# The last units of two projections, taken one block of tokens at a time, with the norm behind them

## The chip, the cores and the metric

The kernel runs on one core of a Trainium2 chip. Its time is the device time of one execution in microseconds (us); lower is better. TensorE (PE) multiplies, VectorE (DVE) and ScalarE (ACT) work on vectors, GpSimd (POOL) does a few of them and issues some transfers, SyncE (SP) issues the large ones.

## The reference, cut to what matters

An encoder of two layers over 256 tokens of width 1024, in float32. Each layer has a mixer (three branches, gated and merged) and a feed-forward part: dense in layer 0, eight experts with top-2 routing in layer 1. What matters here is where the residual x is completed and normalised:

```python
for l in range(DEPTH):
    h = rmsnorm(x, g_mix[l])
    ...
    x = x + merged @ w_o[l]
    h = rmsnorm(x, g_ffn[l])
    if l % 2 == 0:
        x = x + swiglu(h, ffn_w1[i], ffn_w3[i], ffn_w2[i])
    else:
        x = x + moe_ffn(h, moe_router[i], moe_w1[i], moe_w3[i], moe_w2[i])
return rmsnorm(x, g_final)
```

`rmsnorm` divides each token by the root of its mean square over 1024 features and multiplies by a gain.

## The kernel before

**Data.** X holds the residual, tokens on the 128 partitions, in two blocks of tokens (b = 0, 1) with 1024 columns each, which are handled in two halves of 512. Each matrix product is made of three (`mm3`): operands are split into a rounded part (`hi`) and a remainder (`lo`), and hi*hi, hi*lo and lo*hi are added up. Weights come in units of 1 MB (512 rows by 512 columns as a rule; the last of the dense stage have 256 rows). SyncE loads unit u into one of 4 raw buffers when unit u-4 is done (`unit_done`), ScalarE rounds it (L782, `whi`, 3 buffers, so it waits for unit u-3), VectorE makes the remainder (L1132, `wlo`), TensorE multiplies. Each engine follows its own list in order; the semaphores between them are written by hand, and so is the place of every step in each list.

**Units.** Layer 0's mixer has units 0 to 33, the last four of which are w_o: halves 0 and 1 of the first 512 rows (30, 31), then of the other 512 (32, 33). Units 34 to 69 are the dense stage: six steps of 512 hidden columns (256 in the last), w1 and w3, then w2, one step behind; units 68 and 69 are the two halves of the last w2. Unit 70 is the first of layer 1's mixer, whose last four are w_o again. After them the expert stage has a ring of its own.

**The last two units.** `token_unit` (L1679) multiplies one unit for block 0 and then for block 1: the order at the end of w_o is unit 32 for block 0, unit 32 for block 1, unit 33 for block 0, unit 33 for block 1. With `tell` it counts `first_block` after block 0. VectorE adds each of the four sums (b, half) to X (L1438 for w_o, L1465 for the dense stage) and counts `x_ready`, half 0 for both blocks first.

**Norm.** ScalarE squares the four parts of X with a sum (L798); VectorE adds the two halves of the sums (L1148), ScalarE takes the root (L802), VectorE the reciprocal (L1150), each in one instruction for both blocks. VectorE scales block 0 into xn in two parts (L1156), ScalarE block 1 (L809). TensorE turns xn with transposes (L1726), 8 tiles for each block, the two blocks of a tile one after the other, into PSUM (`small`, where the dense stage's sums lie too), counting `norm_turned` after each two tiles. ScalarE rounds the turned tiles with the gain (L816), VectorE makes the remainders (L1170), and the next stage's products can start. `busy(n)` (L1741) issues n products of identity and table whose result nobody reads, which fill time in which TensorE has nothing to do:

```python
if n == 2:
    pe.wait_ge(fh_ready, FSTEPS)
    busy(3, big[1][:, 1, :])
    pe.wait_ge(x_ready, 8)
```

norm(1) follows layer 0's w_o, norm(2) the dense stage. Between the last units and the adds VectorE makes, by its list, the remainder of the unit after them (34, or 70). When layer 0's w_o is added, GpSimd writes 16 blocks of zeros of 512 KB to memory (it waits for `x_ready` 4); after the dense stage it issues layer 1's small loads (`x_ready` 8).

**Before the experts.** After layer 1's w_o, X itself is turned (16 transposes, L1726; fillers `busy(1)` before them), ScalarE and VectorE copy the turned tiles with the gain in turn (L1072 and L1480), and TensorE multiplies them by the router (L1991). Routing and the gathering of tokens follow, and then the first expert unit. The squares for norm(3) are taken by ScalarE around those copies (L1066).

Of the kernel before, what the change touches and what calls it, by code (L numbers as in the profile page):

```python
# [188 lines left out]
def encoder(nc, ins, out):  # L189
    ctx = ExitStack()  # L190
    with ctx:
# [217 lines left out]
        xn_ready = [sem(f"xn_ready{b}") for b in range(NB)]  # L409
        xg_ready = sem("xg_ready")  # L410
# [239 lines left out]
        def _(pool):  # L650
# [46 lines left out]
            for b in range(NB):  # L697
                pool.wait_ge(xn_ready[b], 7)
                pool.tensor_tensor(xn[:, b, :], xn[:, b, :], gffn[:, :], ALU.mult).then_inc(xg_ready, 1)
# [49 lines left out]

        def norm_place(n, k):  # L750
# [20 lines left out]
        def _(act):  # L771
# [14 lines left out]
            def norm_stats(n, ready=None, count=0):  # L786
# [275 lines left out]
            def squares(half):  # L1062
                for b in range(NB):
                    act.wait_ge(x_ready, 8 + 2 * half + b + 1)
# [10 lines left out]
            act.wait_ge(var_ready, 4)  # L1075
# [18 lines left out]
            def last_scale(b):  # L1094
                act.wait_ge(var_ready, 4 + b + 1)
# [19 lines left out]
        def _(dve):  # L1115
# [20 lines left out]
            def norm(n, gain=None):  # L1136
# [10 lines left out]
                dve.wait_ge(ss_ready, n + 1)  # L1147
                dve.tensor_tensor(nvar[:, n, :], nss[:, n, 0, :], nss[:, n, 1, :], ALU.add).then_inc(var_ready, 1)  # L1148
                dve.wait_ge(sd_ready, n + 1)
                dve.reciprocal(nrs[:, n, :], nsd[:, n, :]).then_inc(rs_ready, 1)  # L1150
                dve.wait_ge(rs_ready, n + 1)
# [67 lines left out]

            def mixer(l):  # L1220
                u0 = l * LAYER0_UNITS
                norm(2 * l, R_MIX + KD * l)
# [208 lines left out]
                for g in (G_O, G_O + 1):  # L1431
                    for b in range(NB):
                        if b == 0:
                            dve.wait_ge(first_block, 4 * l + g - G_O + 1)
                        else:
                            dve.wait_ge(unit_done, group_end(l, g))
                        part = X[:, b, 512 * (g - G_O):512 * (g - G_O) + 512]
                        dve.tensor_tensor(part, part, big[g % 2][:, b, :], ALU.add).then_inc(x_ready, 1)  # L1438

            def dense():  # L1440
                norm(1, R_FFN)
# [16 lines left out]
                for half in range(2):  # L1458
                    for b in range(NB):
                        if b == 0:  # L1460
                            dve.wait_ge(first_block, 2 + half + 1)
                        else:
                            dve.wait_ge(unit_done, LAYER0_UNITS - 1 + half)
# [679 lines left out]
```

## Time and profile before

| | us |
|---|---|
| median of 3 runs | 1650.73 |
| lowest, highest | 1650.01, 1652.11 |
| profiled execution | 1649.36 |
| its span, first to last instruction | 1647.7 |
| TensorE busy | 1623.6 (99%) |
| VectorE busy | 1253.3 (76%) |
| ScalarE busy | 1045.6 (63%) |
| mean granted TensorE clock | 0.996 |

The span is the time from the first to the last instruction of one profiled execution; busy times are shares of it. The granted clock is the share of full speed that the chip gave TensorE. A timeline lists instructions in order of start, several of one line merged (x4), and in brackets the idle time of the engine before them with the instruction that ended it.

### The profile page before, as it was taken

The page shows a single profiled execution, that of the slowest core. Times are in us where ns is not written, and L with a number is a line of the kernel's source. Part 1 is how long each engine was busy: PE and PEld are TensorE (multiplying, and loading weights), DVE is VectorE, ACT ScalarE, POOL GpSimd, SP SyncE. Part 2 cuts the span into 40 slices and gives each one's busy share as a digit, 9 for nine tenths or more (in the row PEclk, how much of TensorE's full clock was granted, in tenths as well). Part 3 has the DMA queues.
Part 4 walks back from the last instruction along what each step waited for, and adds up shares of the span by engine and source line. Part 5 has one row for each costly group of instructions (what it writes and reads, how often), then busy time and mean ns, then how long its engine had stood idle before and what let it go on. Part 6 is the DMA issues. An engine that isn't in the chain of part 4 may idle for free.

```text
span 1647.7 us, 22770 instructions
## 1 busy us (share of the span) xinstructions
PE 1623.6 (99%) x8939; PEld 1400.6 (85%) x8939; DVE 1253.3 (76%) x929; ACT 1045.6 (63%) x927; POOL 118.6 (7%) x92
## 2 busy tenths in 40 slices
PE   8999999999999999999999999999999999999998
PEld 6899989999898999777888888888888888888886
DVE  5755575454557567699888898888988988988996
ACT  4464645433534564676777776877776876877775
POOL 1000002000000000022100100100100000001450
PEclk8999999999999999999999999999999999999999
DMA  7644459554754446999999999999999999999980
GB/s 265 200 148 136 153 182 355 187 194 143 243 179 150 142 145 212 412 359 408 387 399 361 390 387 368 393 382 368 398 377 364 401 379 363 404 376 366 415 354 26
DMA packets 162622, 488.98 MB, mean 297 GB/s; under 512 B 8192, under 2 KB 12512, under 8 KB 162560
## 3 DMA queue, kind: packets, MB, share of 16 engines
q1 hardware_dynamic: 154416, 459.05, 75.2%
q0 software_dynamic: 7552, 27.89, 4.7%
q10 hardware_dynamic: 592, 1.16, 0.2%
q8 instruction: 45, 0.74, 0.2%
q14 instruction: 17, 0.14, 0.0%
HBM read 471.82 MB, written 16.25 MB: 296 GB/s over the span
## 4 chain that ended last, share of the span: by engine, by line
PE 91%; DVE 4%; ACT 2%; DMA 2%; issue 1%; POOL 0%; ACTq 0%; DVEq 0%; POOLq 0%
PE big L1675 21%; PE big L1677 21%; PE big L1676 21%; PE small L1675 7%; PE small L1677 7%; PE small L1676 7%; PE small L1726 2%; DVE elo L1217 2%; DMA raw<-ffn_w 1%; ACT ehi L985 1%; ACT whi L782 1%; PE big L1726 1%; DMA lqk<-diff_lk 0%; PE small L1975 0%; DVE wlo L1132 0%
## 5 line engine op out<-in xcount | busy, mean ns | idle before, releaser
L1217 DVE TENSOR_TENSOR elo<-eraw,ehi 128x2048 fp32r<-128x2048 f32 x336 | 774.5, 2325 | 97.4 <-ACT ehi L985 94.5
L985 ACT ACTIVATE ehi<-eraw 128x2048 fp32r<-128x2048 f32 x336 | 641.7, 1918 | 239.9 <-PE big L1677 136.4
L1132 DVE TENSOR_TENSOR wlo<-raw,whi 128x2048 fp32r<-128x2048 f32 (+2 forms) x104 | 230.0, 2218 | 191.7 <-ACT whi L782 191.6
L1675 PE MATMUL big<-ehi,hehi 128*128 128x512 f32 x896 | 351.5, 392 | 4.0 <-DVE elo L1217 3.4
L782 ACT ACTIVATE whi<-raw 128x2048 fp32r<-128x2048 f32 (+2 forms) x104 | 192.4, 1859 | 250.1 <-PE big L1677 177.3
L1677 PE MATMUL big<-ehi,helo 128*128 128x512 f32 x896 | 348.9, 389 | 0.0
L1676 PE MATMUL big<-elo,hehi 128*128 128x512 f32 x896 | 348.7, 389 | 0.0
L1675 PE MATMUL big<-hhi,whi 128*128 128x256 f32 x864 | 246.8, 286 | 2.2 <-DVE wlo L1132 0.8
L1677 PE MATMUL big<-hhi,wlo 128*128 128x256 f32 x864 | 244.5, 283 | 0.0
L1676 PE MATMUL big<-hlo,whi 128*128 128x256 f32 x864 | 244.4, 283 | 0.0
L1675 PEld LDWEIGHTS big<-ehi,hehi 128*128 128x128 f32 x896 | 168.2, 188 | 40.2 <-DVE elo L1217 4.5
L1677 PEld LDWEIGHTS big<-ehi,helo 128*128 128x128 f32 x896 | 168.2, 188 | 35.4
L1676 PEld LDWEIGHTS big<-elo,hehi 128*128 128x128 f32 x896 | 168.3, 188 | 34.0
L1675 PEld LDWEIGHTS big<-hhi,whi 128*128 128x128 f32 x864 | 165.7, 192 | 4.7 <-issue 2.0
L1676 PEld LDWEIGHTS big<-hlo,whi 128*128 128x128 f32 x864 | 165.8, 192 | 0.6 <-issue 0.5
L1677 PEld LDWEIGHTS big<-hhi,wlo 128*128 128x128 f32 x864 | 165.7, 192 | 0.0
L1675 PE MATMUL small<-ehi,eahi 128*128 128x512 f32 x384 | 150.2, 391 | 0.0
L1677 PE MATMUL small<-ehi,ealo 128*128 128x512 f32 x384 | 149.7, 390 | 0.0
L1676 PE MATMUL small<-elo,eahi 128*128 128x512 f32 x384 | 149.4, 389 | 0.0
L1677 PEld LDWEIGHTS small<-ehi,ealo 128*128 128x128 f32 x384 | 72.1, 188 | 15.2
L1676 PEld LDWEIGHTS small<-elo,eahi 128*128 128x128 f32 x384 | 72.1, 188 | 14.8
L1675 PEld LDWEIGHTS small<-ehi,eahi 128*128 128x128 f32 x384 | 72.1, 188 | 14.8
(353 smaller groups left out, 1766.0 us busy)
## 6 DMA issues: line engine op xcount, KB each, us to landing
eraw<-moe_w SPq DMA_DIRECT2D x336, 1024.0 KB, 6.3
raw<-ffn_w SPq DMA_DIRECT2D x30, 1024.0 KB, 5.0
raw<-w_gate SPq DMA_DIRECT2D x24, 1024.0 KB, 5.0
raw<-w_in SPq DMA_DIRECT2D x20, 1024.0 KB, 5.1
raw<-w_branch SPq DMA_DIRECT2D x12, 1024.0 KB, 5.0
raw<-w_o SPq DMA_DIRECT2D x8, 1024.0 KB, 5.1
xs_all<-zeros POOLq DMA_DIRECT2D x12, 512.0 KB, 8.8
xn<-xs_all POOLq DMA_DIRECT2D x8, 512.0 KB, 6.8
```

The source lines that it names most:

```text
L782: act.activation(whi[u % HI][:, 0:kt, 0:cols], raw[u % RAW][:, 0:kt, 0:cols], ACT.Copy).then_inc(hi_ready, 1)
L985: act.activation(ehi[HI_OF[n]][:, :], eraw[n % RING][:, :], ACT.Copy).then_inc(ehi_ready, 1)
L1132: dve.tensor_tensor(wlo[u % RAW][:, 0:kt, 0:cols], raw[u % RAW][:, 0:kt, 0:cols], whi[u % HI][:, 0:kt, 0:cols].bitcast(F32), ALU.subtract) ...
L1217: dve.tensor_tensor(elo[n % RING][:, :], eraw[n % RING][:, :], ehi[HI_OF[n]][:, :].bitcast(F32), ALU.subtract).then_inc(elo_ready, 1)
L1675: pe.matmul(o, sh, mh, start=start, stop=False, **kw)
L1676: pe.matmul(o, sh, ml, start=False, stop=False, **kw)
L1677: return pe.matmul(o, sl, mh, start=False, stop=stop, **kw)
L1726: return pe.transpose(o, src, ident[0:n, 0:n])
```

## The change

The last two units of w_o (both layers) and of the dense stage are multiplied by a new function, `token_pair`: block 0 for both halves, then block 1 for both halves. `first_block` is counted after each half of block 0 and `unit_done` after each of block 1, so that the first unit of a pair is counted as done after its second block. VectorE adds block 0's two halves to X first, then block 1's. In norm(1) and norm(2) the sum, the root, the reciprocal and the scaling are done for block 0 and then for block 1, on VectorE with the adds in between, and the adds are moved into `norm`. ScalarE scales one half of block 1, VectorE the other. TensorE turns all tiles of block 0, waits for all of X, issues two fillers in place of three, and turns block 1. Before the experts it turns block 0's tiles of X, the first five without waiting for block 1, and then block 1's; the filler there goes. Counts of semaphores follow.

```diff
@@ -788,25 +795,25 @@
                 act.activation(warm[:, n:n + 1], eps[:, :], ACT.Sqrt)
-                for half in range(2):
-                    for b in range(NB if n else 1):
+                for b in range(NB if n else 1):
+                    for half in range(2):
...
-                            act.wait_ge(ready, count + 2 * half + b + 1)
+                            act.wait_ge(ready, count + 2 * b + half + 1)
                         part = slice(512 * half, 512 * half + 512)
                         i = act.activation(xn[:, b, part], X[:, b, part], ACT.Square,
                                            accum_out=nss[:, n, half, b:b + 1])
-                i.then_inc(ss_ready, 1)
-                act.wait_ge(var_ready, n + 1)
-                act.activation(nsd[:, n, :], nvar[:, n, :], ACT.Sqrt, scale=1.0 / D, bias=eps[:, :]).then_inc(sd_ready, 1)
+                    i.then_inc(ss_ready, 1)
+                    act.wait_ge(var_ready, stat(n, b))
+                    of = slice(b, b + 1) if n else slice(0, NB)
+                    act.activation(nsd[:, n, of], nvar[:, n, of], ACT.Sqrt, scale=1.0 / D, bias=eps[:, :]).then_inc(sd_ready, 1)
...
             def norm(n, gain, ready=None, count=0):
-                    act.wait_ge(rs_ready, n + 1)
-                    for part in (slice(0, 512), slice(512, 1024)):
-                        act.activation(xn[:, 1, part], X[:, 1, part], ACT.Copy, scale=nrs[:, n, 1:2]).then_inc(xn_ready[1], 1)
+                    act.wait_ge(rs_ready, stat(n, 1))
+                    act.activation(xn[:, 1, 0:512], X[:, 1, 0:512], ACT.Copy, scale=nrs[:, n, 1:2]).then_inc(xn_ready[1], 1)
...
@@ -1059,9 +1066,9 @@
+            def squares(b):
+                for half in range(2):
+                    act.wait_ge(x_ready, 8 + 2 * b + half + 1)
                     part = slice(512 * half, 512 * half + 512)
                     i = act.activation(xn[:, b, part], X[:, b, part], ACT.Square, accum_out=nss[:, 3, half, b:b + 1])
                 return i
...
@@ -1144,17 +1151,33 @@
-                for part in (slice(0, 512), slice(512, 1024)):
-                    for b in range(1 if n else NB):
-                        dve.tensor_scalar(xn[:, b, part], X[:, b, part], nrs[:, n, b:b + 1], None,
-                                          ALU.mult).then_inc(xn_ready[b], 1)
...
+                else:
+                    for b in range(NB):
+                        for half in range(2):
+                            added(b, half)
+                        dve.wait_ge(ss_ready, stat(n, b))
+                        dve.tensor_tensor(nvar[:, n, b:b + 1], nss[:, n, 0, b:b + 1], nss[:, n, 1, b:b + 1],
+                                          ALU.add).then_inc(var_ready, 1)
+                        dve.wait_ge(sd_ready, stat(n, b))
+                        dve.reciprocal(nrs[:, n, b:b + 1], nsd[:, n, b:b + 1]).then_inc(rs_ready, 1)
+                        dve.wait_ge(rs_ready, stat(n, b))
+                        for part in (slice(0, 512), slice(512, 1024))[b:]:
+                            dve.tensor_scalar(xn[:, b, part], X[:, b, part], nrs[:, n, b:b + 1], None,
+                                              ALU.mult).then_inc((xn_ready[0], xn_late)[b], 1)
...
@@ -1217,9 +1240,31 @@
...
+            def mixed(l):
+                def add(b, half):
+                    if b == 0:
+                        dve.wait_ge(first_block, 4 * l + half + 1)
+                    else:
+                        dve.wait_ge(unit_done, group_end(l, G_O + half))
+                    part = X[:, b, 512 * half:512 * half + 512]
+                    dve.tensor_tensor(part, part, big[half][:, b, :], ALU.add).then_inc(x_ready, 1)
+                return add
+            def fed(b, half):
+                if b == 0:
+                    dve.wait_ge(first_block, 2 + half + 1)
+                else:
+                    dve.wait_ge(unit_done, LAYER0_UNITS - 1 + half)
+                part = X[:, b, 512 * half:512 * half + 512]
+                dve.tensor_tensor(part, part, small[:, 2 * b + half, :], ALU.add).then_inc(x_ready, 1)
...
@@ -1428,17 +1473,12 @@
-                for g in (G_O, G_O + 1):
                     for b in range(NB):
-                        if b == 0:
-                            dve.wait_ge(first_block, 4 * l + g - G_O + 1)
-                        else:
-                            dve.wait_ge(unit_done, group_end(l, g))
-                        part = X[:, b, 512 * (g - G_O):512 * (g - G_O) + 512]
-                        dve.tensor_tensor(part, part, big[g % 2][:, b, :], ALU.add).then_inc(x_ready, 1)
+                        for half in range(2):
+                            mixed(l)(b, half)
...
             def dense():
-                norm(1, R_FFN)
+                norm(1, R_FFN, mixed(0))
...
@@ -1676,7 +1708,21 @@
+            def token_pair(us, outs, ahi, alo, k0, first):
+                for b in range(NB):
+                    for half, u in enumerate(us):
+                        _, kt, cols = units[u]
+                        if b == 0:
+                            pe.wait_ge(lo_ready, u + 1)
+                        for k in range(kt):
+                            i = mm3(outs[half][b][:, 0:cols], ahi[:, k0 + k, b * P:b * P + P], alo[:, k0 + k, b * P:b * P + P],
+                                    whi[u % HI][:, k, 0:cols], wlo[u % RAW][:, k, 0:cols],
+                                    first and k == 0, k == kt - 1)
+                        i.then_inc((first_block, unit_done)[b], 1)
+            def token_unit(u, outs, ahi, alo, k0, first, last):
                 _, kt, cols = units[u]
...
@@ -1744,23 +1788,44 @@
             def norm(n):
+                if n == 2:
+                    pe.wait_ge(x_ready, 6)
+                elif n:
+                    wait_out(0, *(f"{n}{j}" for n in ("PV", "DT") for j in range(2)))
...
+                for k in range(KD):
+                    if k % 4 == 0:
+                        pe.wait_ge(xn_ready[0], 2 * n + 1 + k // 4)
+                    if n == 2 and k == 4:
+                        pe.wait_ge(x_ready, 8)
+                    turn(norm_place(n, k)[:, 0:P], xn[:, 0, k * P:k * P + P])
                 if n == 2:
                     pe.wait_ge(fh_ready, FSTEPS)
-                    busy(3, big[1][:, 1, :])
-                    pe.wait_ge(x_ready, 8)
-                elif n:
-                    wait_out(0, *(f"{n}{j}" for n in ("PV", "DT") for j in range(2)))
-                    busy(3)
+                else:
+                    pe.wait_ge(x_ready, 4)
+                busy(2, big[1][:, 1, :])
                 for k in range(KD):
-                    q, j = k // 2, k % 2
-                    if n == 0 and q == 3:
-                        pe.wait_ge(pcol_ready, 1)
-                    for b in range(NB):
-                        if k % 4 == 0:
-                            pe.wait_ge(xn_ready[b], 2 * n + 1 + k // 4)
-                        i = turn(norm_place(n, k)[:, P * b:P * b + P], xn[:, b, k * P:k * P + P])
-                    if j:
+                    if k == 0:
+                        pe.wait_ge(xn_ready[1], n + 1)
+                    if k == 4:
+                        pe.wait_ge(xn_late, n + 1)
+                    i = turn(norm_place(n, k)[:, P:2 * P], xn[:, 1, k * P:k * P + P])
+                    if k % 2:
                         i.then_inc(norm_turned, 1)
...
@@ -1935,13 +2000,14 @@
                 branch(l, 4)
                 pe.wait_ge(br_read[1], 3 * l + 2)
                 branch(l, 5)
-                for j in range(2):
-                    for g in (G_O, G_O + 1):
-                        if not j:
-                            pe.wait_ge(br_read[g % 2], 3 * l + 3)
-                        pe.wait_ge(mlo_ready, 2 * l + j + 1)
-                        token_unit(l * LAYER0_UNITS + group_units(g)[j], [big[g % 2][:, b, :] for b in range(NB)],
-                                   hhi, hlo, 4 * j, j == 0, j == 1, tell=bool(j))
+                for g in (G_O, G_O + 1):
+                    pe.wait_ge(br_read[g % 2], 3 * l + 3)
+                    pe.wait_ge(mlo_ready, 2 * l + 1)
+                    token_unit(l * LAYER0_UNITS + group_units(g)[0], [big[g % 2][:, b, :] for b in range(NB)],
+                               hhi, hlo, 0, True, False)
+                pe.wait_ge(mlo_ready, 2 * l + 2)
+                token_pair([l * LAYER0_UNITS + group_units(g)[1] for g in (G_O, G_O + 1)],
+                           [[big[half][:, b, :] for b in range(NB)] for half in range(2)], hhi, hlo, 4, False)
...
@@ -1957,10 +2023,15 @@
                     if f:
                         pe.wait_ge(flo_ready, f)
+                        if f == FSTEPS:
+                            token_pair([LAYER0_UNITS - 2, LAYER0_UNITS - 1],
+                                       [[small[:, 2 * b2 + half, :] for b2 in range(NB)] for half in range(2)],
+                                       fhi[(f - 1) % 2], flo[(f - 1) % 2], 0, False)
+                            continue
...
@@ -1979,12 +2050,13 @@
             dense()
             mixer(1)
             wait_out(1, *(f"{n}{j}" for n in ("PV", "DT") for j in range(2)))
-            busy(1)
-            pe.wait_ge(x_ready, 12)
+            pe.wait_ge(x_ready, 10)
             for k in range(KD):
-                for b in range(NB):
-                    i = turn(turned_place(k)[:, P * b:P * b + P], X[:, b, k * P:k * P + P])
-                i.then_inc(norm_turned, 1)
+                if k == 5:
+                    pe.wait_ge(x_ready, 12)
+                turn(turned_place(k)[:, 0:P], X[:, 0, k * P:k * P + P])
+            for k in range(KD):
+                turn(turned_place(k)[:, P:2 * P], X[:, 1, k * P:k * P + P]).then_inc(norm_turned, 1)
```

## Rows read from the trace of the kernel before

**Rows 1.** The page, busy time: us, share of the span, instructions.

```profile
PE 1623.6 (99%) x8939; PEld 1400.6 (85%) x8939; DVE 1253.3 (76%) x929; ACT 1045.6 (63%) x927; POOL 118.6 (7%) x92
```

**Rows 2.** TensorE's waits, 445 to 1640: us in total, times, longest.

```profile
PE big L1675 <- DVE elo L1217: 3.4, 4, 1.3
```

**Rows 3.** Timeline of TensorE, first seam: start, us, engine, line; in brackets idle before.

```profile
244.80 0.39 PE L1677 MATMUL big<-whi,hlo 128*128 128x512 f32 x1
...
245.03 2.73 PE L1744 MATMUL small<-tab 128*128 128x512 f32 x6
...
248.06 2.00 PE L1726 MATMUL small<-tab,xn 128*128 128x128 f32 x16 [0.30 <-DVE xn L1156]
...
250.29 0.36 PE L1675 MATMUL big<-hhi,whi 128*128 128x256 f32 x1 [0.23 <-DVE hlo L1170]
```

**Rows 4.** Timelines of VectorE, then ScalarE, first seam.

```profile
230.71 4.49 DVE L1132 TENSOR_TENSOR wlo<-raw,whi 128x2048 fp32r<-128x2048 f32 x2 [0.58 <-ACT whi L782]
...
239.79 0.69 DVE L1438 TENSOR_TENSOR X<-X,big 128x512 f32<-128x512 f32 x1 [0.54 <-PE big L1677]
...
245.23 0.69 DVE L1438 TENSOR_TENSOR X<-X,big 128x512 f32<-128x512 f32 x1 [2.03 <-PE big L1677]
...
247.43 0.96 DVE L1156 TENSOR_SCALAR xn<-X,nrs 128x512 f32<-128x512 f32 x2
...
247.43 1.33 ACT L809 ACTIVATE xn<-X,nrs 128x512 f32<-128x512 f32 x2 [0.23 <-DVE nrs L1150]
...
248.79 3.04 ACT L816 ACTIVATE hhi<-small,pcol 128x256 fp32r<-128x256 f32 x8
```

**Rows 5.** Windows: length, busy of each engine, TensorE clock, DMA share, GB/s.

```profile
245.00:246.00 1.00, 1.00 (x4) 0.49 (x3) 0.69 (x1) 0.05 (x1) 0.02 (x1) 1.00 0.00 0
...
278.00:280.00 2.00, 2.00 (x19) 2.00 (x18) 1.21 (x1) 1.40 (x2) 0.00 (x0) 1.00 1.05 407
```

**Rows 6.** Timeline of TensorE, dense stage, two waits.

```profile
274.36 0.35 PE L1675 MATMUL big<-hhi,whi 128*128 128x256 f32 x1 [0.77 <-ACT fsil L964]
...
281.14 0.39 PE L1675 MATMUL big<-hhi,whi 128*128 128x256 f32 x1 [0.80 <-DVE wlo L1132]
```

**Rows 7.** Timeline of TensorE, second seam.

```profile
440.11 2.73 PE L1744 MATMUL big<-tab 128*128 128x512 f32 x6
...
443.75 2.00 PE L1726 MATMUL small<-tab,xn 128*128 128x128 f32 x16 [0.91 <-DVE xn L1156]
...
445.98 0.36 PE L1675 MATMUL big<-hhi,whi 128*128 128x256 f32 x1 [0.23 <-DVE hlo L1170]
```

**Rows 8.** Timeline of VectorE, second seam.

```profile
436.87 2.29 DVE L1132 TENSOR_TENSOR wlo<-raw,whi 128x2048 fp32r<-128x2048 f32 x1 [5.07 <-ACT whi L782]
...
439.08 2.47 DVE L1465 TENSOR_TENSOR X<-X,small 128x512 f32<-128x512 f32 x4
...
442.39 0.16 DVE L1148 TENSOR_TENSOR nvar<-nss 128x2 f32<-128x2 f32 x1 [0.84 <-ACT xn L798]
...
443.12 0.88 DVE L1156 TENSOR_SCALAR xn<-X,nrs 128x512 f32<-128x512 f32 x2
```

**Rows 9.** Timelines of TensorE, then ScalarE, third seam.

```profile
667.86 1.02 PE L1744 MATMUL small<-tab 128*128 128x512 f32 x2
...
668.80 1.09 PE L1726 MATMUL small<-tab,X 128*128 128x128 f32 x8
...
670.70 3.62 PE L1991 MATMUL small<-hT,rt 128*8 128x256 f32 x16
...
669.27 0.91 ACT L1072 ACTIVATE hT<-small,pcol 128x256 f32<-128x256 f32 x2 [4.24 <-PE small L1726]
```

**Rows 10.** Start of the kernel: TensorE's timeline, then windows.

```profile
11.77 0.27 PE L1726 MATMUL big<-tab,prow 96*128 96x96 f32 x1 [4.37 <-DMA prow<-gm_b_s]
...
12.00:13.00 1.00, 0.66 (x2) 0.36 (x2) 0.60 (x4) 0.57 (x2) 0.00 (x0) 0.78 1.06 412
...
22.00:24.00 2.00, 1.82 (x12) 1.47 (x11) 2.00 (x6) 1.99 (x6) 0.00 (x0) 0.80 1.00 408
```

More of the change, by code:

```diff
@@ L1134, in split_to, with norm @@
                     split[0] += 1
-            def norm(n, gain=None):
+            def norm(n, gain=None, added=None):
                 if n == 0:
@@ L1146, in norm @@
                     dve.tensor_copy(rb4[:, :, :], bc(rb[:, :], 2, [BUCKETS, HEADS, P])).then_inc(rb4_ready, 1)
[L1147 to L1151, printed above, removed]
+                if n == 3 or n == 0:
+                    dve.wait_ge(ss_ready, stat(n, 0))
+                    dve.tensor_tensor(nvar[:, n, :], nss[:, n, 0, :], nss[:, n, 1, :], ALU.add).then_inc(var_ready, 1)
+                    dve.wait_ge(sd_ready, stat(n, 0))
+                    dve.reciprocal(nrs[:, n, :], nsd[:, n, :]).then_inc(rs_ready, 1)
+                    dve.wait_ge(rs_ready, stat(n, 0))
@@ L1457, in dense @@
                 split_to(LAYER0_UNITS)
-                for half in range(2):
-                    for b in range(NB):
[L1460 to L1463, printed above, removed]
-                        part = X[:, b, 512 * half:512 * half + 512]
-                        dve.tensor_tensor(part, part, small[:, 2 * b + half, :], ALU.add).then_inc(x_ready, 1)
             dve.memset(eps[:, :], EPS).then_inc(eps_ready, 1)
@@ L1677, in mm3 @@
                 return pe.matmul(o, sl, mh, start=False, stop=stop, **kw)
-            def token_unit(u, outs, ahi, alo, k0, first, last, tell=False):
+            def token_pair(us, outs, ahi, alo, k0, first):
+                for b in range(NB):
+                    for half, u in enumerate(us):
[8 more added lines that the diff above has]
+            def token_unit(u, outs, ahi, alo, k0, first, last):
                 _, kt, cols = units[u]
@@ L1747, in norm @@
                 if n == 2:
-                    pe.wait_ge(fh_ready, FSTEPS)
-                    busy(3, big[1][:, 1, :])
-                    pe.wait_ge(x_ready, 8)
+                    pe.wait_ge(x_ready, 6)
                 elif n:
                     wait_out(0, *(f"{n}{j}" for n in ("PV", "DT") for j in range(2)))
-                    busy(3)
-                for k in range(KD):
-                    q, j = k // 2, k % 2
-                    if n == 0 and q == 3:
-                        pe.wait_ge(pcol_ready, 1)
-                    for b in range(NB):
-                        if k % 4 == 0:
-                            pe.wait_ge(xn_ready[b], 2 * n + 1 + k // 4)
-                        i = turn(norm_place(n, k)[:, P * b:P * b + P], xn[:, b, k * P:k * P + P])
-                    if j:
+                if n == 0:
+                    for k in range(KD):
+                        if k == 6:
+                            pe.wait_ge(pcol_ready, 1)
+                        for b in range(NB):
+                            if k == 0 or (k == 4 and b == 0):
+                                pe.wait_ge(xn_ready[b], 1 + k // 4)
+                            elif k == 4:
+                                pe.wait_ge(xn_late, 1)
+                            i = turn(norm_place(n, k)[:, P * b:P * b + P], xn[:, b, k * P:k * P + P])
+                        if k % 2:
+                            i.then_inc(norm_turned, 1)
+                    return
+                for k in range(KD):
+                    if k % 4 == 0:
[4 more added lines that the diff above has]
+                if n == 2:
+                    pe.wait_ge(fh_ready, FSTEPS)
+                else:
[7 more added lines that the diff above has]
+                    i = turn(norm_place(n, k)[:, P:2 * P], xn[:, 1, k * P:k * P + P])
+                    if k % 2:
                         i.then_inc(norm_turned, 1)
```

29 lines of the change are left out of this document (16 added, 13 removed).

## The prediction

> **What bounds the kernel now.** I read the page's busy shares first, then its chain, then TensorE's waits, and last the timelines of the three places that the change touches. TensorE is busy for 99% of the span [rows 1], and the chain runs along it nearly throughout. After the second place TensorE hardly waits for anyone until the end: the largest wait from there on is 3.4 us in four pieces, on expert weight remainders [rows 2]. So a microsecond lost before TensorE's next long run of products is lost at the end, unless a later transfer is what TensorE would have waited for. The three places are the seams at which the residual X is completed. Seam 1 (norm(1), after layer 0's w_o): the last product is issued until 245.03, fillers and turns follow, and the first dense product starts at 250.29 [rows 3], 5.26 us later. Seam 2 (norm(2), after the dense stage): 440.11 to 445.98, 5.87 us [rows 7]. Seam 3 (X turned for the router): 667.86 to the first router product at 670.70, 2.84 us [rows 9].
>
> **Seam 1, on TensorE's side.** The products are the same ones in another order. Block 0's sums are then complete two half units earlier, while block 1's last sum still completes at the same moment, so its add still starts at 245.23 and block 1's scale is ready at 247.43, 2.20 us after it [rows 4]. Block 0's whole chain lies under products: its second add started at 239.79 before and still can, its scale is there 2.20 us later at 241.99, and two scaled parts take 0.96 us [rows 4], done before 243, with 2 us to spare. The weight remainder of the last unit is needed 2.7 us earlier (half a unit of 24 products, which are issued 0.23 us apart [rows 3]), and both remainders are done at 235.20 [rows 4] against a need at 245.03 - 8.16 = 236.87: a margin of 1.7 us. What is left after 247.43: ScalarE makes one scaled copy in place of two (1.33 us for two, so 0.67), ready at 248.10. TensorE turns block 0 and runs two fillers in the meantime. The step from a ready part to a turn took 0.15 us (247.43 + 0.48 to 248.06), and at seam 3 two turns released ScalarE 0.47 us after they started (668.80 to 669.27) [rows 3, 4, 9], which gives 248.72 for ScalarE's first rounding, against 248.79 now. Most of what the seam loses in turns was already hidden behind ScalarE's second copy, so the gain is 0.1 us.
>
> **Seam 1, what comes after.** Even that is not kept. When X is complete GpSimd writes 16 blocks of zeros of 512 KB, and the 16 DMA engines are then full: share 1.05 still at 278 to 280 us [rows 5]. TensorE waits in that stretch at 274.36 (0.77 us, for ScalarE, which had stood before it for a weight block to land) and at 281.14 (0.80 us) [rows 6]. TensorE's position at 281 is thus set by bytes queued from 247 on. Unit 36's load is released by unit 32, which counts as done 2.7 us later than before, but the DMA engines are idle at 245 to 246 [rows 5], and that transfer fits there. I take 0 for seam 1, between -0.2 and +0.2.
>
> **Seam 2.** Here the cover is missing. VectorE makes the remainder of unit 70 first (436.87 to 439.08, it waits for ScalarE, which waits for a unit that ends as before), and only then adds to X. Before, the four adds ran in one go (2.47 us, 0.62 each), ScalarE's squares beside them, and one chain of sum, root and reciprocal led to the scale at 443.12 [rows 8]. In the changed order VectorE takes block 0 alone: adds at 439.08 and 439.70, then it stands still in `norm` for ScalarE's square, for the root and for its own reciprocal, with block 1's adds queued behind those waits. Scale of block 0 at 439.70 + 2.20 = 441.90, two scaled parts 0.88, so block 1's adds at 442.78 and 443.40, and its scale at 443.40 + 2.20 = 445.60: 2.48 us later than 443.12. Then ScalarE's copy, 0.67, 446.27. TensorE turns block 0's first four tiles at about 442.5, waits for all of X (443.40 + 0.68 = 444.08) before the other four because they land where block 1's products lie, and runs two fillers of 0.91 us (a third of 2.73 [rows 7]), until about 446.5. Block 1's turns start at 446.5, ScalarE's rounding at 446.97 against 444.45 now (443.12 + 1.33, the two copies of [rows 4]), and the first product moves from 445.98 to about 448.5: +2.5 us. Low end +1.8 (the rounding starts as soon as the one copy is done, 446.27 against 444.45), high end +3.0 (all eight turns of block 1, 1.0 us, stand before it in place of two). Nothing behind it takes it back [rows 2].
>
> The Trainium skill (TensorE: Matmul & The Clock Gate, Architectural detail) says that ScalarE and VectorE are strictly first in, first out. The trace agrees: VectorE stood for 0.84 us before its sum at 442.39 [rows 8]. Were the engine able to pass a waiting instruction, seam 2 would cost nothing and the sum would be -0.5 us.
>
> **Seam 3.** Turns of block 0 now start with the last product, at 667.86; five are done when block 1's last add ends (667.86 + 5 x 0.12 = 668.5 against 668.80, when turns could start before). Three of block 0 and eight of block 1 remain: 11 in place of 16, and 16 took 1.90 us [rows 9], so 0.12 each and 1.31 in all. Router products then start at 668.80 + 1.31 = 670.11 in place of 670.70: -0.6 us at most. The copies of the turned tiles start some 0.3 us later than 669.27, and the first router product needs one, 0.47 us long, so it starts at 670.0 to 670.2. I take -0.5, between -0.6 and 0 (0 if the copies, in pairs of 0.46 us, set the pace). VectorE's routing and the first expert unit follow that chain. The filler of 0.94 us that goes stood beside the wait for X and costs nothing.
>
> **The rest.** Two more sums, roots and reciprocals on one column each, all of them inside the chains above. Layer 1's small loads, which GpSimd issues when X is complete, start 2.5 us later; the middle of the layer wants them.
>
> **Sum.** 0 + 2.5 - 0.5 = +2.0 us, own bounds +1.0 (-0.2 + 1.8 - 0.6) to +3.2 (0.2 + 3.0). The profiled execution took 1649.36 us (span 1647.7), so it would be 1651.4; it is 1.4 us under the median of the runs, 1650.73, so the median comes to 1652.7, with 1651.7 to 1653.9 as its own range.
>
> **Rivals.**
> A, the slower side: the clock falls at seam 2. Before, three fillers followed the last product at once. Now TensorE is empty from 440.11 to 442.5 (2.4 us), turns for 0.5, is empty for 1.1, works 3.3 and is empty for 1 more. In this trace TensorE's granted clock fell from the upper level (2.4 GHz) to the lower (1.2 GHz) between 12 and 13 us, after it had done nothing from 7.4 to 11.77, and came back only between 22 and 24 [rows 10]. Against it: expert stage gaps of 1.3 us cost no clock, and 2.4 is much shorter than 4.4. Price: 0 to half of that stretch of some 10 us, 4.9; I take 2.5, so +4.5 and 1655.2 us. It decides from 2.6 us at the lower level on (1.3 us lost, which with +2.0 passes 3.3). Chance 0.2. The Trainium skill (same page, What's actually happening) has the array throttled by default and activity releasing it; by that alone the thin seam would fall to the lower level, and the sum would be the same +4.5.
> B, faster than before: block 0's chain is covered at seam 2 as well, the case that makes all three seams shorter. It would need block 1's last add at 440.31, 0.2 after the last product; counting back through one add (0.62), two parts (0.88) and 2.20, block 0's second add at 436.6 and VectorE free at 436.0. Unit 70's remainder would have to be done 3.1 us earlier, and [rows 8] show it starting at 436.87. Price: the seam falls from 5.87 to seam 1's 5.26 less 0.1, so -0.7; with -0.5 and up to -0.1 that is -1.3, and 1649.4 us. Chance 0.06.
> C, seam 3 gives nothing (copies set its pace) and seam 2 its high end: +3.0, 1653.7 us. Chance 0.1, next to the forecast and inside its range.
>
> **How the numbers follow.** A measurement of this kernel tells about 0.2% from no change, 3.3 us here, so slower begins at 1654.0 and faster ends at 1647.4. The forecast holds 0.60 and C 0.10, together 0.62 within and 0.08 above. A's 0.20 is 0.18 above and 0.02 within. B's 0.06 lies within. 0.04 is left, set on faster, for a cover at seam 2 together with a gain further on that no row shows. Same 0.70, slower 0.26, faster 0.04. Range: 1649.3 takes B in, 1656.5 most of A.
>
> **What would show it.** Right: in the trace after, first product of layer 1 some 8.3 us after the last dense product (5.87 before), VectorE's adds at seam 2 in two pairs with about 2.5 us between them, block 1's scale 2.5 us later; first dense product 5.1 to 5.3 us after w_o's last, and TensorE's waits near 274 and 281 still there; first router product 2.2 to 2.4 us after the last of w_o. Wrong: four adds in one run at seam 2, or unit 70's remainder out of the way before them, or a granted clock under 1 near 440 to 455.

## The result and the profile after

The changed kernel takes 1653.83 us (median of 12 runs, 1651.62 to 1655.66), the kernel before 1650.33 us (12 runs beside them). The ratio is 1.0021, 95% interval 1.0013 to 1.0028: +3.5 us, between +2.1 and +4.6. The interval does not hold 1, so the changed kernel is slower; by 0.21%, which is at the 0.2% where the prediction lets "slower" begin. The profiled execution has a span of 1651.7 us against 1647.7, +4.0 us.

Seam 1 in the timeline of TensorE of the changed kernel (start, us, line; idle before in brackets):

```profile
244.84 1.03 PE L1770 MATMUL small<-tab,xn 128*128 128x128 f32 x8
245.78 1.98 PE L1788 MATMUL big<-tab 128*128 128x512 f32 x4
248.00 1.09 PE L1770 MATMUL small<-tab,xn 128*128 128x128 f32 x8 [0.24 <-ACT xn L816]
249.98 0.36 PE L1707 MATMUL big<-hhi,whi 128*128 128x256 f32 x1 [0.88 <-DVE hlo L1193]
```

From the end of w_o to the first dense product it takes 5.14 us (5.26 in [rows 3]). The two waits of [rows 6] are still there, the first 0.20 us shorter, the second 0.27 us longer:

```profile
273.86 0.35 PE L1707 MATMUL big<-hhi,whi 128*128 128x256 f32 x1 [0.57 <-ACT fsil L971]
...
280.91 0.39 PE L1707 MATMUL big<-hhi,whi 128*128 128x256 f32 x1 [1.07 <-DVE wlo L1139]
```

and from the end of w_o to the end of the dense stage (440.05) the trace after shows 195.21 us, the trace before 195.08 [rows 3, 7]. In this pair of traces nothing of the 0.12 us is left; what more traces say of it stands under e7.

Seam 2, TensorE:

```profile
439.82 0.39 PE L1709 MATMUL small<-whi,flo 128*128 128x512 f32 x1
442.48 0.72 PE L1770 MATMUL small<-tab,xn 128*128 128x128 f32 x4 [2.27 <-DVE xn L1179]
444.06 1.09 PE L1770 MATMUL small<-tab,xn 128*128 128x128 f32 x4 [0.86 <-DVE X L1263]
444.94 3.62 PE L1788 MATMUL big<-tab 128*128 128x512 f32 x4
448.36 1.70 PE L1770 MATMUL small<-tab,xn 128*128 128x128 f32 x8
450.53 0.36 PE L1707 MATMUL big<-hhi,whi 128*128 128x256 f32 x1 [0.48 <-DVE hlo L1193]
```

The last product is issued until 440.05 and the first of layer 1 comes at 450.53: 10.48 us, against 5.87 [rows 7]. VectorE in the same place:

```profile
436.83 2.29 DVE L1139 TENSOR_TENSOR wlo<-raw,whi 128x2048 fp32r<-128x2048 f32 x1 [5.09 <-ACT whi L789]
439.04 1.28 DVE L1263 TENSOR_TENSOR X<-X,small 128x512 f32<-128x512 f32 x2
441.12 0.16 DVE L1173 TENSOR_TENSOR nvar<-nss 128x1 f32<-128x1 f32 x1 [0.80 <-ACT xn L805]
...
442.64 1.28 DVE L1263 TENSOR_TENSOR X<-X,small 128x512 f32<-128x512 f32 x2
...
445.44 0.48 DVE L1179 TENSOR_SCALAR xn<-X,nrs 128x512 f32<-128x512 f32 x1
```

The four adds that stood in one row [rows 8] are two pairs that begin 3.6 us apart, and between them VectorE waits, sums, takes the reciprocal and scales for block 0. Block 1's scaling starts at 445.44, 5.39 us after the last product; it was 3.01 (443.12 - 440.11). But from there the first product took 5.09 us more, against 2.86. The windows tell why. Their columns are: length, busy time of TensorE, its weight loads, VectorE, ScalarE and GpSimd, granted clock of TensorE, DMA share, GB/s.

```profile
442.00:443.00 1.00, 0.53 (x4) 0.42 (x4) 1.00 (x3) 0.00 (x0) 0.00 (x0) 0.94 1.04 401
443.00:444.00 1.00, 0.20 (x1) 0.00 (x0) 0.91 (x2) 0.65 (x3) 0.00 (x0) 0.50 1.06 365
...
448.00:449.00 1.00, 1.00 (x5) 0.64 (x4) 0.00 (x0) 0.00 (x0) 0.00 (x0) 0.50 0.98 184
449.00:450.00 1.00, 1.00 (x6) 0.81 (x5) 0.10 (x1) 0.97 (x3) 0.00 (x0) 0.65 0.83 313
```

TensorE had been empty for 2.27 us and was turning its four tiles when the clock fell to the lower level at about 442.9 (0.94 is the mean of 442 to 443). It stayed there until about 449.7 (0.65 is the mean of 449 to 450), 6.8 us. The two fillers took 3.62 us at this level (1.88 at the upper one, in e3 below), and block 1's turns stood behind them.

Seam 3, TensorE:

```profile
672.43 0.60 PE L1770 MATMUL small<-tab,X 128*128 128x128 f32 x4
...
673.37 0.55 PE L1770 MATMUL big<-tab,X 128*128 128x128 f32 x3 [0.23 <-DVE X L1252]
...
674.72 3.62 PE L2063 MATMUL small<-hT,rt 128*8 128x256 f32 x16
```

2.29 us against 2.84 [rows 9]. Against the trace before, the changed kernel is behind by 4.55 us at layer 1's first product, by 4.02 at the first router product, and by 4.0 at the end of the span. Seam 3's gain is thus kept to the end: from layer 1's first product on it takes 1201.2 us in place of 1201.7.

### The profile page after: what moved, and what is told of

It reads as the page before. It is cut to its first block, busy times and chain, and to the rows that moved or that the text cites. A ratio compares the mean times of both kernels' runs of the same rounds, so it can differ in the third digit from the quotient of the medians.

```text
span 1651.7 us, 22763 instructions
## 1 busy us (share of the span) xinstructions
PE 1624.2 (98%) x8933; PEld 1401.0 (85%) x8933; DVE 1254.6 (76%) x935; ACT 1044.9 (63%) x927; POOL 116.0 (7%) x92
## 4 chain that ended last, share of the span: by engine, by line
PE 90%; DVE 4%; ACT 2%; DMA 2%; issue 1%; POOL 0%; ACTq 0%; DVEq 0%; POOLq 0%
PE big L1707 21%; PE big L1709 21%; PE big L1708 21%; PE small L1707 7%; PE small L1709 7%; PE small L1708 7%; PE small L1770 2%; DVE elo L1240 2%; DMA raw<-ffn_w 1%; ACT ehi L992 1%; ACT whi L789 1%; PE big L1770 1%; DMA lqk<-diff_lk 0%; DVE wlo L1139 0%; PE small L1908 0%
```

## The experiments

Edits are against the changed kernel where nothing else is said. Ratios are to the kernel before, with the 95% interval; "seam 2" is the time in the run's profile from the moment until which the last dense product is issued (0.23 us after its start) to layer 1's first product.

| run | us (kernel before beside it) | ratio | seam 2, us |
|---|---|---|---|
| e1_seam2_as_before | 1650.07 (1650.53) | 0.9997 [0.9988, 1.0006] | 5.87 |
| e2_pair_one_chain | 1649.87 (1650.53) | 0.9996 [0.9987, 1.0005] | 6.01 |
| e3_fillers | 1651.49 (1650.53) | 1.0006 [0.9997, 1.0015] | 8.17 |
| e4_four_adds | 1650.38 (1650.53) | 1.0000 [0.9991, 1.0009] | 6.58 |
| e5_before_no_fillers | 1651.55 (1650.42) | 1.0006 [0.9997, 1.0015] | 6.94 |
| e6_before_paced | 1648.13 (1650.42) | 0.9987 [0.9978, 0.9996] | 5.98 |
| e7_seams_1_3_paced | 1647.34 (1650.42) | 0.9983 [0.9974, 0.9992] | 6.01 |
| e8_remainder_later | 1651.44 (1650.42) | 1.0009 [0.9999, 1.0018] | 7.19 |
| e9_halved_remainder | 1647.07 (1650.78) | 0.9979 [0.9969, 0.9989] | 5.31 |
| e10_changed_again | 1654.43 (one execution) | | 9.79 |

The intervals are some 1.5 us wide to each side. Where two runs differ by less than that, the verdict below rests on the seams in the traces, which repeat to about 0.1 us: seam 1 takes 5.14 or 5.15 us in the changed kernel and in all eight experiments that have the changed one, seam 3 takes 2.29 or 2.30. The part ahead of seam 1 doesn't repeat like this: the last product of w_o is issued until 244.55 to 247.00 us, and the granted clock over 20 to 40 us is 0.85 to 0.95, whatever the kernel. So seams, and not places in the span, are compared between runs.

**e1_seam2_as_before.** Is the whole loss made at seam 2? Last units, adds, norm(2), fillers and turns are put back there:

```diff
                         if f == FSTEPS:
-                            token_pair([LAYER0_UNITS - 2, LAYER0_UNITS - 1],
...
+                            for half in range(2):
+                                token_unit(LAYER0_UNITS - 2 + half, [small[:, 2 * b2 + half, :] for b2 in range(NB)],
+                                           fhi[(f - 1) % 2], flo[(f - 1) % 2], 0, False, True, tell=True)
```

> The changed kernel with seam 2 (last units of the dense stage, norm(2), its fillers and turns) as in the kernel before; seams 1 and 3 stay changed. Theory (the whole loss is made at seam 2, seam 3 gains 0.55, seam 1 keeps nothing): 0.5 us under the kernel before, ratio 0.9997, seam 2 again 5.9 us long. Rival (part of the loss comes from elsewhere, such as the units that count as done later, or seam 1): 1 us or more above the kernel before.

TensorE in its trace:

```profile
441.12 2.74 PE L1811 MATMUL big<-tab 128*128 128x512 f32 x6
444.76 2.00 PE L1793 MATMUL small<-tab,xn 128*128 128x128 f32 x16 [0.91 <-DVE xn L1186]
446.99 0.36 PE L1728 MATMUL big<-hhi,whi 128*128 128x256 f32 x1 [0.23 <-DVE hlo L1214]
```

It is as expected: seam 2 is the one of before, and the time is 0.5 us under the kernel before. That the changed kernel is slower is due to seam 2: the two intervals, 1.0013 to 1.0028 and 0.9988 to 1.0006, have nothing in common.

**e2_pair_one_chain.** Is it the order of the products, or what follows from them? The pair order stays, and the rest of seam 2 is as before; the cut shows VectorE's part:

```diff
-                if n == 3 or n == 0:
+                if n == 2:
+                    for b in range(NB):
+                        for half in range(2):
+                            added(b, half)
+                if n in (0, 2, 3):
                     dve.wait_ge(ss_ready, stat(n, 0))
```

> As e1, but the last two dense units are multiplied one block at a time (as in the change) and the four adds go block 0 first, in one run; squares, root, reciprocal, scaling, fillers and turns of seam 2 as before. Theory (VectorE's queue in norm(2) costs the time, not the order of the products): the same as e1, ratio 0.9997, seam 2 5.9 us. Rival (the order of the products, or unit 68 counted as done later, delays what follows): 0.5 to 2 us above e1, and a wait for a weight remainder soon after layer 1 begins.

The same time as e1, and the same seam but for 0.14 us (6.01). The order of the products costs no more than that; the loss comes from what was changed behind it: the chains, fillers and turns. e3 and e4 take these apart.

**e3_fillers.** How much of the seam is the clock?

```diff
                 if n == 2:
+                    pe.wait_ge(fh_ready, FSTEPS)
+                    busy(2, big[1][:, 1, :])
                     pe.wait_ge(x_ready, 6)
...
                     if n == 2 and k == 4:
+                        busy(1, big[1][:, 1, :])
                         pe.wait_ge(x_ready, 8)
```

> The changed kernel with fillers at seam 2 where TensorE stood empty: two right behind the last dense product, one between block 0's fourth and fifth turn; the two before block 1's turns stay. Theory (2.4 us of the loss is VectorE's queue, some 2 us the lower clock that follows the empty stretch): clock 1.00 through the seam, first product of layer 1 8.3 us after the last dense one (10.5 in the changed kernel's profile), and 1.9 us above the kernel before, ratio 1.0011. Rival (the clock falls anyhow, or the empty stretch was not its cause): as the changed kernel, ratio 1.0021.

Its seam 2 in the timeline of TensorE, and then the windows over it (columns as above):

```profile
440.75 1.88 PE L1788 MATMUL big<-tab 128*128 128x512 f32 x4
443.20 0.63 PE L1770 MATMUL small<-tab,xn 128*128 128x128 f32 x4 [0.57 <-DVE xn L1179]
...
446.94 1.09 PE L1770 MATMUL small<-tab,xn 128*128 128x128 f32 x8
448.92 0.36 PE L1707 MATMUL big<-hhi,whi 128*128 128x256 f32 x1 [0.89 <-DVE hlo L1193]
```

```profile
442.00:444.00 2.00, 1.43 (x7) 0.69 (x6) 1.60 (x6) 0.29 (x1) 0.00 (x0) 1.00 1.08 401
444.00:446.00 2.00, 1.99 (x8) 0.88 (x7) 0.83 (x4) 1.63 (x5) 1.06 (x2) 1.00 1.00 374
446.00:448.00 2.00, 2.00 (x11) 1.05 (x9) 0.62 (x2) 1.30 (x3) 2.00 (x4) 1.00 0.98 342
```

The clock stays at the upper level and the seam is 8.17 us, 2.3 more than before and 2.3 less than in the changed kernel's profile. So the loss has two parts: 2.3 us with the clock at 1.00, which e4 looks into, and 2.3 us for the clock in that execution. The time is 1.0 us above the kernel before where 1.9 was expected; the interval holds both. VectorE's rows are those of the changed kernel (block 1's scaling 5.42 us after the last product, there 5.39), so it is the clock alone that the fillers mended.

**e4_four_adds.** Does the queue of VectorE set block 1's scale?

```diff
+                    if n == 2:
+                        for b in range(NB):
+                            for half in range(2):
+                                added(b, half)
                     for b in range(NB):
-                        for half in range(2):
+                        for half in range(2 if n == 1 else 0):
                             added(b, half)
...
                 if n == 2:
+                    pe.wait_ge(fh_ready, FSTEPS)
+                    busy(3, big[1][:, 1, :])
...
-                busy(2, big[1][:, 1, :])
+                busy(1 if n == 2 else 2, big[1][:, 1, :])
```

> As e3 (three fillers behind the last product, one before block 1's turns), and VectorE adds all four parts at seam 2 before it takes up block 0's sums. Theory (block 1's adds stand behind VectorE's waits for block 0): block 1's scale about 1.2 us earlier than in e3, seam 2 about 7.1 us long, 0.7 us above the kernel before, ratio 1.0004. Rival (the queue of VectorE does not matter, ScalarE's squares set the pace): as e3, ratio 1.0011.

VectorE in its trace, then ScalarE's root for block 0:

```profile
439.51 2.47 DVE L1267 TENSOR_TENSOR X<-X,small 128x512 f32<-128x512 f32 x4
441.90 0.15 DVE L1177 TENSOR_TENSOR nvar<-nss 128x1 f32<-128x1 f32 x1
...
444.37 0.49 DVE L1183 TENSOR_SCALAR xn<-X,nrs 128x512 f32<-128x512 f32 x1
...
442.09 0.29 ACT L810 ACTIVATE nsd<-nvar,eps 128x1 f32<-128x1 f32 x1 [0.53 <-DVE nvar L1177]
```

Last product at 440.54, block 1's scaling 3.83 us later; in e3 it came 5.42 us after (446.17 against 440.75). 1.6 us are gained where I expected 1.2, and the seam is 6.58 us against 7.1 expected: 1.6 of the 2.3 us come from block 1's adds standing behind VectorE's waits. The 0.7 us that are left over e1 are the second round of sum, root and reciprocal. The root for block 0 stands between ScalarE's squares of the two blocks. ScalarE waits 0.53 us for VectorE's sum and takes 0.29 us for the root, and block 1's squares and scaling come 0.82 us later against the last product than in e1 (3.83 against 3.01 us). The clock was at 1.00 throughout.

**e5_before_no_fillers.** Does an empty stretch alone bring the clock down? In the kernel before:

```diff
-                    busy(3, big[1][:, 1, :])
```

> The kernel before without its three fillers at seam 2: TensorE stands empty for 3.6 us behind the last dense product, and VectorE's and ScalarE's chain is the one of before. Theory (the empty stretch alone brings the clock down): granted clock 0.5 for some us between 443 and 450, and 1 to 3 us above the kernel before, ratio 1.0006 to 1.0018, though no chain is longer. Rival (the clock holds over 3.6 us, the changed kernel lost it for the thin work after the gap): clock 1.00, ratio 1.0000.

The timeline of TensorE in its trace, then windows of the same place:

```profile
439.83 0.39 PE L1677 MATMUL small<-whi,flo 128*128 128x512 f32 x1
443.70 3.65 PE L1726 MATMUL small<-tab,xn 128*128 128x128 f32 x16 [3.48 <-DVE xn L1156]
447.00 0.56 PE L1675 MATMUL big<-hhi,whi 128*128 128x256 f32 x1
```

```profile
442.00:443.00 1.00, 0.00 (x0) 0.00 (x0) 0.29 (x2) 0.61 (x3) 1.00 (x3) 0.79 1.04 338
...
448.00:449.00 1.00, 1.00 (x6) 1.00 (x6) 1.00 (x3) 1.00 (x2) 0.00 (x0) 0.50 1.01 420
449.00:450.00 1.00, 1.00 (x9) 1.00 (x8) 0.14 (x1) 1.00 (x2) 0.00 (x0) 0.79 0.96 397
```

It does. The chain on VectorE and ScalarE takes as long as before (4.03 us from the first add to the first scaling), yet from the first turn to the first product it takes 3.3 us in place of 2.2, and the products after it run at the lower level until about 449.4. The last dense product is issued until 440.06, so the seam is 6.94 us against 5.87: 1.1 us are lost in it. From the first product to the end another 1.1 us are lost (1202.8 us against 1201.7). In time it is 1.1 us above the kernel before, with an interval that also holds no change; the traces show the loss.

**e6_before_paced.** Are the waits near 274 and 281 due to the zeros? In the kernel before:

```diff
             for s in range(SLOTS + 1):
+                if s and s % 3 == 0:
+                    pool.wait_ge(fh_ready, s // 3)
                 pool.dma_start(xs_all[SLOT * s:SLOT * s + SLOT, :], zeros[:, :]).then_inc(zeroed, 16)
+            pool.wait_ge(fh_ready, 4)
             for s in range(NE - 1, SLOTS):
```

> The kernel before with GpSimd's 16 blocks of zeros spread over the dense stage (three at a time, each group behind a step's hidden product) in place of all at once after layer 0's w_o. Theory (TensorE's waits near 274 and 281, 1.6 us together, come from those transfers): both gone, 1.6 us under the kernel before, ratio 0.9990. Rival (the waits have another cause, or move to later weight units): ratio 1.0000.

The timeline of TensorE in its trace, at the first dense product and at the fillers behind the last:

```profile
251.53 0.35 PE L1678 MATMUL big<-hhi,whi 128*128 128x256 f32 x1 [0.23 <-DVE hlo L1173]
...
439.22 2.73 PE L1747 MATMUL big<-tab 128*128 128x512 f32 x6
```

187.69 us from one to the other, against 189.82 (250.29 to 440.11): both waits (1.57 us) are gone, and 0.56 us more, whose place is open. The time falls by 2.1 us by the ratio (0.7 to 3.6).

**e7_seams_1_3_paced.** e1 with the same edit.

> e1 (seams 1 and 3 changed, seam 2 as before) with the zeros paced as in e6. Theory (seam 1's 0.12 us was swallowed by the waits near 274 and 281): with these waits gone the seam keeps it, so from the last product of w_o to the end of the dense stage 0.12 us less than in e6, and the time 0.65 us under e6, 2.2 us under the kernel before, ratio 0.9986. Rival: no more than seam 3's 0.55 under e6.

From the end of w_o (244.95) to the end of the dense stage (437.76) its trace shows 192.81 us, that of e6 192.96, and that of e9 below, which has the changed seam 1 too, 192.90. The direction is the one expected, but single executions scatter more than that. In the kernels with the waits the same stretch takes 195.08 us (before) and 195.51 (e5) with the old seam 1, and 194.87 to 195.21 with the changed one (changed kernel, e1 to e4, e8, e10). So whether the waits swallow the 0.12 us is not settled. The time, 1647.34 us, is 0.8 us under e6, beside which it ran; the intervals overlap.

**e8_remainder_later.** Is it unit 70's remainder that uncovers block 0? On top of e3:

```diff
                             dve.tensor_scalar(xn[:, b, part], X[:, b, part], nrs[:, n, b:b + 1], None,
                                               ALU.mult).then_inc((xn_ready[0], xn_late)[b], 1)
+                    if n == 2:
+                        split_to(LAYER0_UNITS)
...
-                split_to(LAYER0_UNITS)
+                split_to(LAYER0_UNITS - 1)
```

> e3 with VectorE's remainder of unit 70 made behind block 1's scaling instead of ahead of block 0's adds. Theory (that remainder holds VectorE until 1.1 us before the last dense product and so uncovers block 0's chain): block 0's adds start 1.4 us earlier, block 1's scale 1.2 us earlier than in e3; the remainder then stands before the first hlo, so seam 2 comes to about 7.2 us against 8.2. Rival (block 0's chain waits for ScalarE or the products): adds no earlier, seam 2 longer than e3's by the 2.2 us of the remainder.

VectorE in its trace (the last product is issued until 440.22):

```profile
437.70 0.69 DVE L1265 TENSOR_TENSOR X<-X,small 128x512 f32<-128x512 f32 x1 [0.67 <-PE small L1711]
439.86 0.16 DVE L1173 TENSOR_TENSOR nvar<-nss 128x1 f32<-128x1 f32 x1 [1.47 <-ACT xn L805]
...
444.18 0.49 DVE L1179 TENSOR_SCALAR xn<-X,nrs 128x512 f32<-128x512 f32 x1
444.58 2.29 DVE L1139 TENSOR_TENSOR wlo<-raw,whi 128x2048 fp32r<-128x2048 f32 x1
```

Block 0's adds come as soon as the products are there, block 1's scaling 3.96 us after the last product (5.42 in e3), and the seam is 7.19 us as expected, with the remainder now ahead of the first hlo. Even so block 0 isn't covered: its sum at 439.86 had waited 1.47 us for ScalarE, whose first square could only start at 438.50, behind unit 70's rounding (435.17 to 437.09) and a table load. ScalarE in the same trace:

```profile
437.10 1.28 ACT L797 ACT_TABLE_LOAD   x1
...
438.50 0.61 ACT L805 ACTIVATE xn<-X 128x512 f32<-128x512 f32 x1
```

In time e8 and e3 can't be told apart (ratios 1.0009 and 1.0006), so the microsecond rests on the traces alone, in which both take 1201.2 us from layer 1's first product to the end.

**e9_halved_remainder.** The version that all this points to: seams 1 and 3 changed, zeros paced, at seam 2 the pair order with one chain, and unit 70's remainder in two halves between the adds (`part_lo` makes one half):

```diff
+                if n == 2:
+                    added(0, 0)
+                    part_lo(LAYER0_UNITS, 0)
+                    added(0, 1)
+                    part_lo(LAYER0_UNITS, 1)
+                    added(1, 0)
+                    added(1, 1)
...
-                split_to(LAYER0_UNITS)
+                split_to(LAYER0_UNITS - 1)
```

> Seams 1 and 3 changed, zeros paced, and seam 2 as in e2 (pair order, one chain), with VectorE making unit 70's remainder in two halves between the adds: add, half, add, half, two adds. Theory (the chain of seam 2 starts late because the whole remainder stands before the first add): the last add starts 0.3 to 0.4 us after the last dense product instead of 0.8, seam 2 about 5.5 us against 5.9, and the time 0.4 us under e7, 3.1 us under the kernel before, ratio 0.9981. Rival (the table load and ScalarE's squares set the pace): seam 2 5.9 to 6.0 us, time as e7, ratio 0.9983.

VectorE in its trace, the remainder's two halves, adds and scaling:

```profile
434.88 1.22 DVE L1162 TENSOR_TENSOR wlo<-raw,whi 128x1024 fp32r<-128x1024 f32 x1
...
436.62 1.22 DVE L1162 TENSOR_TENSOR wlo<-raw,whi 128x1024 fp32r<-128x1024 f32 x1
437.75 1.28 DVE L1299 TENSOR_TENSOR X<-X,small 128x512 f32<-128x512 f32 x2
...
440.56 0.89 DVE L1201 TENSOR_SCALAR xn<-X,nrs 128x512 f32<-128x512 f32 x2
```

Scaling starts 2.45 us after the last product (438.11), the seam is 5.31 us, and 1647.07 us (ratio 0.9979) is the lowest time of all: 3.7 us under the kernel before beside it, and 6.8 under the changed one, which ran at another time. That it beats e7 (0.9983) is not shown by the times, whose intervals overlap; the 0.7 us between their seams is from the traces.

**e10_changed_again.** No edit.

> The changed kernel once more, one profile: does the clock fall at seam 2 in every execution? Theory: TensorE stands empty for 2.3 us and works little for the next two, so it falls again or not by the moment at which the gap comes; with the fall seam 2 is 9.5 to 10.5 us long, without it 8.2 us. Rival (it always falls there): 10.5 us again.

Windows of its seam 2:

```profile
445.00:446.00 1.00, 0.13 (x1) 0.16 (x2) 0.72 (x2) 0.84 (x3) 0.00 (x0) 0.95 1.09 354
...
448.00:449.00 1.00, 1.00 (x2) 0.33 (x1) 0.00 (x0) 0.00 (x0) 1.00 (x2) 0.50 0.96 332
449.00:450.00 1.00, 1.00 (x5) 0.42 (x4) 0.00 (x0) 0.00 (x0) 0.17 (x1) 0.85 1.12 236
```

The clock fell again, but later (at about 445.9) and for 3.4 us in place of 6.8, and the seam is 9.79 us, 0.7 less. That this execution was longer all the same is due to its start: the last product of w_o is issued until 247.00, against 244.84, with a granted clock of 0.85 over 20 to 40 us against 0.92. Two profiled executions of two fell at seam 2, for different lengths. For the 12 timed ones only the mean clock is known, from 0.996 (1651.62 us) to 0.992 (1655.12 us), and it can't tell seam 2 from the start: e1's profiled execution has 0.994 with 1.00 throughout seam 2.

## Why the prediction was right or wrong

The time lies in the stated range, 0.2 us under the 1654.0 where "slower" was to begin. The sum that led to 1652.7 was right in its three terms and left out a fourth, which I had as rival A with a chance of 0.2. The difference, +3.5 us, lies above the sum's own bounds (+1.0 to +3.2). That 1653.83 still falls within the forecast's 1651.7 to 1653.9 is luck: the kernel before came out at 1650.33 here, 0.4 us under the 1650.73 from which I started. And layer 1's first product came 10.48 us after the last dense one, where I had put 8.3.

- **Seam 1: right as far as can be told.** 5.14 us, as worked out (-0.1). The waits at 274 and 281 are there as long as the zeros go out in one go, and e6 and e7 show that they come from these transfers. That they swallow the 0.12 us is not shown: the stretch behind the seam scatters by 0.3 us and more. No harm from unit 36's later load is to be seen. One reading was off without effect: the add at 239.79 in the kernel before was block 1's first, and block 0's second started at 242.51. In the changed order block 0's second add takes that earlier place (239.59).
- **Seam 2, VectorE's queue: right, size 2.3 us for 2.5.** Block 1's scaling came 2.38 us later (2.48 predicted). e4 shows that 1.6 us of it are the chain between the adds (the rest is the second round of root and reciprocal), and e8 that unit 70's remainder is what first holds VectorE. The strict order itself is better seen in the trace after than in the wait of 0.84 us that I gave for it, behind which nothing was ready: block 1's products were complete at 440.2, and its adds began at 442.64. What I had missed under B: without that remainder ScalarE's rounding of unit 70 and its table load are next in the way, so B needed more than a free VectorE.
- **Seam 2, the clock: wrong.** The step that failed is the weighing of rival A, "2.4 is much shorter than 4.4": it took the longest empty stretch as what counts. What the runs showed in its place: in the changed kernel the clock fell during the four turns behind 2.27 us empty, in e10 after a second empty stretch, later and for a shorter time. The price of A was right (2.5 taken; 2.3 in the profile, 1.6 in e10), its mechanism too: e3 brings the clock back with fillers alone, and e5 takes it from the kernel before by taking out its three fillers.
- **Seam 3: right,** 0.55 us for 0.5.
- **The sum.** 2.3 - 0.55 + 0 and 1.6 to 2.3 for the clock make +3.4 to +4.1, against +3.5 (2.1 to 4.6) measured. What the forecast named as a sign against it, a granted clock under 1 near 440 to 455, is what the trace shows.

Open: in what share of executions the clock falls at seam 2, since only two were profiled there.

## What to carry to other kernels

Splitting a chain into blocks pays only where the first block's chain fits under work that is still running. Look up in the trace when the engine that must run it comes free: 1 us before the last product was too late here for a chain of 3.7 us, and then the second block's first step queued behind the first block's last. Where a seam is rearranged, look at what TensorE does in each new gap, and leave the fillers where the gap begins, not where the last wait ends. And don't count on a gain ahead of a stretch that waits for transfers: here it could not even be told whether seam 1's 0.12 us survived it. Spreading those transfers took 2.1 us out of that stretch, more than the 0.7 us of seams 1 and 3 together.

## What the runs showed of the hardware

The lower clock level came on after less idleness than I had thought. In e5 the last product was issued until 440.06 and the level fell at about 442.6, with nothing run in between. In the changed kernel it fell at about 442.9, behind 2.27 us empty and 0.4 us of turns; in e10 at about 445.9, behind 2.25 us empty, four turns and another 0.96 us empty. Gaps of 1.35 us (before 750.15 in the kernel before) and of 1.05 us (e2) left it at 1.00. It stayed low for 6.8 us in the first two and for 3.4 us in e10. With fillers that left no gap over 0.89 us (e3) the granted clock stayed at 1.00. ScalarE took root and square in turn without a table load between them: in the changed kernel's trace its first square of block 1 (443.35) follows the root of block 0 (441.31) with none. The table load ahead of them took 1.28 us in e8, and the next activation began right behind it (437.10 to 438.38, then 438.39).
